# A third buffer for the output projection's weight halves, a bias rounded later, half of a rounding moved to GpSimd, and a first gather by feature groups

## What is computed

```python
y = _rms(y.reshape(...)) * out_norm_g
x = x + gate1 * (y @ w_out)                       # the output projection

h2 = rms_norm(x, norm2_g) * (1 + scale2) + shift2
logits = (xt @ router_w + router_b).astype(jnp.float32)
top_vals, top_idx = lax.top_k(logits, TOP_K)      # 4 of 32 experts
def expert_step(acc, params):
    u = xt @ w1 + b1
    glu = jnp.minimum(u[:, ::2], SWIGLU_LIMIT)
    lin = jnp.clip(u[:, 1::2], -SWIGLU_LIMIT, SWIGLU_LIMIT)
    a = glu * jax.nn.sigmoid(SWIGLU_ALPHA * glu) * (lin + 1)
    out = a @ w2 + b2
    return acc + gate_e[:, None] * out.astype(jnp.float32), None
```

## Time and profile before

| | |
|---|---|
| median of 3 runs | 1646.22 us (1643.47 to 1648.41) |
| the profiled execution | 1649.03 us, its span 1647.3 us |
| busy of the span | PE 93%, DVE 41%, ACT 28%, POOL 6% |
| moved by DMA | 534.24 MB, mean 324 GB/s |
| mean granted TensorE clock | 0.985 of full speed |

### The profile page before, as it was taken

How to read it: one execution, slowest core, us unless ns; L and a number is a source line. 1 busy time by engine, 2 the same in 40 slices (tenths; PEclk the granted TensorE clock), 3 DMA queues, 4 the chain that set the end, 5 groups by cost and what they waited for, 6 DMA issues and landing times. The chain is left out here.

```text
span 1647.3 us, 21485 instructions
## 1 busy us (share of the span) xinstructions
PE 1532.7 (93%) x8573; PEld 869.0 (53%) x8573; DVE 667.4 (41%) x960; ACT 454.0 (28%) x754; POOL 99.8 (6%) x114
## 2 busy tenths in 40 slices
PE   6999899999999988999998889886999999999998
PEld 3888633333333323333333323222858998789986
DVE  3576522232222222322221222223866565465654
ACT  3574411101111110111110101002865444354443
POOL 4032000000000000000000000000530000400000
PEclk8999899999999999999999999999999999999999
DMA  9977689999999999999999999999436555466540
GB/s 365 333 220 282 246 351 427 427 422 409 426 426 426 425 427 426 427 421 426 425 428 426 426 426 427 426 426 346 140 103 218 181 191 191 128 198 192 187 154 26
DMA packets 109695, 534.24 MB, mean 324 GB/s; under 512 B 6769, under 2 KB 69896, under 8 KB 83040
## 3 DMA queue, kind: packets, MB, share of 16 engines
q1 hardware_dynamic: 107600, 529.97, 81.1%
q0 software_dynamic: 1936, 1.98, 0.4%
HBM read 530.87 MB, written 1.05 MB: 323 GB/s over the span
## 5 line engine op out<-in xcount | busy, mean ns | idle before, releaser
L936 PE MATMUL ps<-ring,arena 128*64 128x512 f32 x2040 | 490.5, 606 | 21.8 <-DMA ring<-in_w_mlp 19.8
L936 PEld LDWEIGHTS ps<-ring,arena 128*64 128x64 f32 x2040 | 130.1, 137 | 261.7 <-issue 211.7
L954 PE MATMUL ps<-ring,arena 128*64 128x512 f32 x1024 | 230.9, 597 | 19.0 <-DMA ring<-in_w_mlp 11.6
L1546 DVE TENSOR_TENSOR wl<-ring,wh 128x1024 fp32r<-128x1024 f32 x132 | 162.0, 1232 | 135.2 <-ACT wh L2424 135.2
L541 PE MATMUL ps<-hth,wh 128*128 128x256 f32 x704 | 200.2, 284 | 1.9 <-DVE htl L2215 1.9
L542 PE MATMUL ps<-htl,wh 128*128 128x256 f32 x704 | 197.9, 281 | 0.0
L543 PE MATMUL ps<-hth,wl 128*128 128x256 f32 x704 | 197.3, 280 | 0.0
L2015 DVE TENSOR_TENSOR arena<-ps,arena 128x1024 f32<-128x1024 f32 x68 | 83.3, 1224 | 257.3 <-PE ps L961 250.6
L2424 ACT ACTIVATE wh<-ring 128x1024 fp32r<-128x1024 f32 x132 | 139.3, 1060 | 148.0 <-PE ps L543 148.0
L954 PEld LDWEIGHTS ps<-ring,arena 128*64 128x64 f32 x1024 | 74.1, 137 | 168.7 <-issue 142.3
L2040 DVE TENSOR_TENSOR arena<-ps,arena 128x512 f32<-128x512 f32 x34 | 23.5, 691 | 337.7 <-PE ps L954 334.5
(11 more groups left out here) (442 smaller groups left out, 1838.0 us busy)
## 6 DMA issues: line engine op xcount, KB each, us to landing
ring<-in_w_mlp SPq DMA_DIRECT2D x190, 2048.0 KB, 24.3
ring<-in_w_ada SPq DMA_DIRECT2D x24, 1024.0 KB, 11.0
ring<-in_ffn_w_gate SPq DMA_DIRECT2D x22, 1024.0 KB, 5.4
ring<-in_ffn_w_up SPq DMA_DIRECT2D x22, 1024.0 KB, 5.4
ring<-in_ffn_w_down SPq DMA_DIRECT2D x22, 1024.0 KB, 4.9
ring<-in_w_in SPq DMA_DIRECT2D x10, 768.0 KB, 12.2
ring<-in_w_in_ab SPq DMA_DIRECT2D x6, 1024.0 KB, 11.6
ring<-in_w_out SPq DMA_DIRECT2D x4, 1024.0 KB, 5.1
```

Source lines behind the costliest of these rows:

```text
L936: t = pe.matmul(PS[64 * g:64 * g + 64, HB[hb][ns], :], x[:, k8, :], u[:, f:f + 512], start=False, stop=k8 == 7)
L954: t = pe.matmul(PS[64 * g:64 * g + 64, 3, :], a4[:, kc, 64 * kg:64 * kg + 64], u[:, c, g * 512:(g + 1) * 512], start=k8 == 0, stop=k8 == 7)
L1546: dve.tensor_tensor(l, src, h.bitcast(F32), ALU.subtract).then_inc(*V.tick((st, "lo", n)))
```

## The change

Four edits:

- `out_bufs` gets a third pair of buffers, at `o_P + 1024`, which the mixer has left by then. `hi` of half n now waits for half n - 3.
- ACT rounds halves 2 to 5 in one run, then copies the gate row, then halves 6 and 7, and `B1S` behind them. DVE does its part of `B1S` behind half 7.
- `HL` of token tile 1 is written by GpSimd and no more by DVE: one instruction multiplies x by `rr[1]` into a new buffer `XR`, two subtract `HH`.
- The first gather goes by feature groups through the function `gather(b, kk, bank)`: groups 0 and 1 before the bias and `first_unit(0)`, groups 2 and 3 behind it. PE waits for all of `HL` before the first matmul.

```diff
         out_bufs = [tuple(rounded(f"wo{q}{n}", at_arena + 4 * (at + 1024 * n), 1024) for n in range(2))
-                    for q, at in enumerate((o_qk, o_ws + 2048))]
+                    for q, at in enumerate((o_qk, o_ws + 2048, o_P + 1024))]
...
             pe.wait_ge(*done(("ST", 0)))
             pe.wait_ge(*done(("HH", 1)))
-            for k in range(8):
-                for i in range(2):
-                    pe.matmul(PS[:, 4 + k // 2, (k % 2) * 256:(k % 2) * 256 + 256], HH[:, i, k * 128:(k + 1) * 128],
-                              ST[:, i, :], start=i == 0 and k % 2 == 0, stop=False)
-            for k in range(8):
-                for i in range(2):
-                    pe.wait_ge(*done(("HL", i)))
-                    t = pe.matmul(PS[:, 4 + k // 2, (k % 2) * 256:(k % 2) * 256 + 256], HL[:, i, k * 128:(k + 1) * 128],
-                                  ST[:, i, :], start=False, stop=i == 1 and k % 2 == 1)
-                if k % 2:
-                    t.then_inc(*P.tick(("gathered", 0, k // 2)))
+            for i in range(2):
+                pe.wait_ge(*done(("HL", i)))
+            gather(0, 0, 4)
+            gather(0, 1, 5)
...
             first_unit(0)
+            gather(0, 2, 6)
+            gather(0, 3, 7)
...
-            for n in range(2, 6):
+            for n in range(2, 8):
                 lo("out", n)
             for g in range(2):
                 p0 = 32 + 64 * g
                 dve.wait_ge(*done("B1H"))
                 dve.tensor_tensor(B1S[p0:p0 + 32, :], B1raw[p0:p0 + 32, :], B1S[p0:p0 + 32, :].bitcast(F32),
                                   ALU.subtract).then_inc(*V.tick("B1S"))
-            lo("out", 6)
-            lo("out", 7)
...
             dve.tensor_copy(most, cmax).then_inc(*V.tick("cnt"))
-            h_rest(1, 0, 1024)
             dve.wait_ge(*done("pos turned"))
...
-            hi("out", 2)
-            hi("out", 3)
+            for n in range(2, 6):
+                hi("out", n)
             for hf in range(2):
                 act.wait_ge(*done(("gate1", hf)))
                 act.activation(G1B[:, hf * 512:(hf + 1) * 512], PS[:, 6 + hf, :], ACT.Copy).then_inc(*S.tick(("G1B", hf)))
+            hi("out", 6)
+            hi("out", 7)
             act.wait_ge(s_load["b1"], 64)
             act.wait_ge(*done(("y turned", 3)))
             act.activation(B1S, B1raw, ACT.Copy).then_inc(*S.tick("B1H"))
-            for n in range(4, 8):
-                hi("out", n)
...
+            pool.wait_ge(*done(("x1", 1, 1)))
+            pool.wait_ge(*done(("rec", "n2", 1)))
+            pool.tensor_scalar(XR, X[:, 1, :], rr[1], None, ALU.mult).then_inc(*G.tick("XR"))
+            pool.wait_ge(*done("XR"))
+            pool.wait_ge(*done(("HH", 1)))
+            for c in range(2):
+                pool.tensor_tensor(apart(HL[:, 1, :], 0, 1024)[:, :, c, :], pairs(XR, 0, 1024)[:, :, c, :],
+                                   apart(HH[:, 1, :].bitcast(F32), 0, 1024)[:, :, c, :], ALU.subtract).then_inc(
+                    *G.tick(("HL", 1)))
```

More of the change, by code:

```diff
@@ L385, in build @@
         B1raw = v1(o_P + 3072, 1024)
+        XR = v1(o_P + 2048, 1024)
         HH, HL = (rounded_at(n, o, 2048).rearrange("p (t n) -> p t n", t=2)
```

## The result

| | before | with the change |
|---|---|---|
| median of 14 runs each, us | 1648.43 (1643.47 to 1651.76) | 1642.64 (1639.09 to 1645.53) |
| profiled execution, its span | 1649.03, 1647.3 | 1642.65, 1640.8 |
| mean granted clock | 0.985 | 0.986 |
| first product of half 0 | 156.53 | 156.74 |
| first quarter of x | 183.01 | 177.33 |

The ratio of the times is 0.9971 [0.9962, 0.998]: 0.29% faster, 4.8 us of 1648.43, with an interval (3.3 to 6.3 us) that lies on both sides of the 4.9 us that I had called the limit of what can be told. The forecast was 1642.2, which was 4.0 us less than the median of 1646.22 known then; that of before now came out 2.2 us higher.

What follows compares the result with a forecast made beforehand. Expert weight transfers were taken to bound the kernel, so its time follows the issue at 209.50 us. Terms -5.8 + 0 + 0 + 1.8 = -4.0 us, from 1646.22 to 1642.2 us; range 1638.8 to 1646.6.

Steps and rivals of the forecast that it cites:

- Term 1: Output projection: with PE's pauses at halves 4 and 7 gone, x starts at about 177.2 us, -5.8 us.
- The cover for `b1`: Output projection: the new order needs `b1` at 173.4 us; it landed at 168.9, 4.5 us of cover.
- rival D: Output projection: `b1` lands later as transfers share the DMA engines, eating the whole gain; 1646.2 us, chance 0.10.
- Terms 2 and 3: DVE losing `h_rest(1)` behind `ST`, and the gather's new order on PE: nothing on the chain waits, 0 each.
- Term 4: Routing: GpSimd's two subtractions shut out small DVE instructions, `ST` 1.8 us later; nothing charged for `XR`; +1.8 us.
- rival E: Gather: PE idles longer before it and its clock stays at half up to the issue; +2.7, 1648.9 us, chance 0.08.
- Rival B: Routing: GpSimd's work costs DVE nothing; -5.8, 1640.4 us, chance 0.15.
- rival C: Routing: `XR` shuts DVE out too, holding `h_rest` of tile 0, about +3.2; sum -2.6, 1643.6 us, chance 0.17.
- The row at 1402 us: Profile: a DVE subtraction took its normal 1.23 us beside a GpSimd multiply, so nothing was charged for `XR`.
- the rule of the sum: Expert stage: kernel time moves microsecond for microsecond with the expert transfer issued at 209.50 us before.

Runs made afterwards that it cites:

- r2: The kernel before with only the projection's part (third buffer, new order on ACT and DVE), GpSimd and gather as before: ratio 0.9957.
- r5: The kernel before with the third buffer alone, ACT and DVE in their old order: 1643.28 us.
- r6: The kernel before with the new order on ACT and DVE alone, two buffers: 1641.07 us.
- r4: The changed kernel with the old gather, first_unit(0) again behind all 32 gather matmuls: ratio 0.9961.
- r8: r4 with one more wait, so that GpSimd's two subtractions run behind `ST`, beside the gather: 1640.62 us.
- r9: r2 with four extra matmuls of unused result before PE's wait for the top 4, to keep PE awake: ratio 0.9954.
- r10: r2's program again, unchanged: ratio 0.9966.
- r1: The changed kernel again, as it is: ratio 0.9964.
- r3: The kernel before with only GpSimd's part (`XR`, two subtractions, DVE without h_rest(1)), projection and gather as before: ratio 1.0007.
- r7: The changed kernel with `XR` made by a GpSimd multiply of two tensor inputs instead of one by a scalar: 1642.81 us.

## Why the prediction held

**Term 1, the projection, -5.8: right.** x came 5.68 us earlier (5.89 counted), by the steps given: no pause at half 4, none at half 7, half 7's tiles and `B1S` meeting at 177.1 to 177.3. r2 shows it alone, r5 and r6 show both of its causes apart. That 2.0 us lay beyond the two pauses, from the half clock in 170 to 180 us, is right for most of it: PEclk went from 0.83 to 1.00. Before, the clock was at half from 172.1 to 175.5, over 3.3 us of PE's work, of which half, 1.6 us, was lost; where the other 0.4 comes from, I have not traced. The cover for `b1` held, so rival D fell.

**Terms 2 and 3, 0 and 0: right.** r4 shows the second directly, 48.45 against 48.43 and 48.75. The first was not tried by itself; in r8 `h_rest(1)` is away from DVE too and nothing on the chain before `ST` is shorter than in r2.

**Term 4, GpSimd, +1.8: the mechanism and the place right, the size a little low.** `XR` took 2.85 us where 2.9 was taken. The two instructions grew by 0.84 and 0.99 (1.06 and 1.21 against 0.22), where the text had 0.8 and 1.0. But from the reciprocal to `ST` the change is 2.22 us longer than before, 2.45 longer than r2. What the sum left out is PE's part of that chain, the places: three pairs of small matmuls between `chosen` and `ST`. From the last choice to DVE's next instruction they took 1.81 us in the change (191.28 to 193.09), 1.41 before. PE's timeline of the change there, and the window:

```profile
191.56 0.64 PE L890 MATMUL ps<-arena 128*128 128x32 f32 x2 [4.16 <-DVE arena L1952]
```
```profile
190.00:192.00 2.00, 0.43 (x2) 0.44 (x3) 1.93 (x5) 0.00 (x0) 1.17 (x1) 0.50 0.18 74
```

PE came out of a pause of 4.16 us, before 2.33, and the granted clock had already fallen to its half level, 1.2 GHz, in it. The step takes 1.17 to 1.23 us at the full clock (r2, r5, r6, r9), 1.4 where the clock falls within it (before, r10) and 1.81 at half. It was at half in all five profiles with the longer pause (the change, r1, r3, r4: 4.16 us, r7: 4.48), and once with the short one of 2.33 (r8). So the argument against rival E, that these matmuls "stay as they are", failed, in another place than E had: the half clock costs 0.4 us ahead of `ST`, not 6.7 behind it. That the longer pause brings it on is likely by these counts, but r8 shows that it isn't the only way. What the mis-sized term comes to at the issue lies between 1.4 and 3.2 us: 1.9 by r3 against before, 2.9 to 3.2 by the change and r1 against r2, 1.4 to 1.7 against r10.

**Rival B fell** (the subtractions cost what they were charged), and **rival C fell**: `h_rest` of tile 0 beside `XR` took 0.91 us, 0.87 before. The Trainium skill (page SBUF — State Buffer, section SBUF: two separate sides) says that a VectorE instruction with two SBUF inputs is fully blocked by a GpSimd instruction that reads SBUF and started before it. By that rule `XR` would hold `h_rest` in the change as it does in r7. It doesn't: the rule agrees with the trace for GpSimd's two-input instructions (1.26 us in place of 0.51 beside the multiply of r7, 1.06 and 1.21 in place of 0.22 beside the subtractions of the change), and does not hold for a multiply by one scalar for each row (2.85 us beside two DVE instructions of normal length). The row at 1402 us, by which the prediction decided, had told this right.

**From the gather on: not quite 1:1.** The clock behind the gather, on which E hung, did move the sum, in the other direction. From the gather's start to the issue before took 11.85 us, the change 11.07, because the full clock came back 2.6 us after the gather's start and not 5.1. The last two columns of the table bear this out: r9, with none of it at half, takes 9.66; each microsecond at half should add half of one, and 9.66 plus half of the last column gives 10.9 for r2 (10.65), 11.0 for the change (11.07), 11.5 for r1 (11.42), 12.2 and 12.3 for before and r10 (11.85, 11.89), and fits all twelve to 0.4 us. When the clock comes back differs between two profiles of one program (r2 and r10), so that these 0.8 us are not the change's.

**From the issue to the end: the rule is borne out.** This stretch took 1437.8 us before, 1435.7 with the change. Part of the difference stands at the end of the expert stage. PE's timeline of before there, and then that of the change:

```profile
1134.17 3.26 PE L954 MATMUL ps<-ring,arena 128*64 128x512 f32 x8 [0.62 <-ACT arena L2734]
...
1146.46 0.73 PE L1242 MATMUL ps<-obh,sgt 64*128 64x512 f32 x4 [3.09 <-DVEq L549]
```
```profile
1129.87 1.94 PE L955 MATMUL ps<-ring,arena 128*64 128x512 f32 x8 [0.62 <-ACT arena L2727]
...
1139.26 0.73 PE L1238 MATMUL ps<-obh,sgt 64*128 64x512 f32 x4 [1.79 <-DVEq L550]
```

Before ran part of its last expert at half clock and was 2.87 us longer from the issue to the first product behind the experts (936.96 against 934.09). No edit touches that, and it is not the change's. The same eight matmuls in r2, and in r10, which is the same program:

```profile
1127.86 1.94 PE L954 MATMUL ps<-ring,arena 128*64 128x512 f32 x8 [0.62 <-ACT arena L2732]
```
```profile
1128.94 3.46 PE L954 MATMUL ps<-ring,arena 128*64 128x512 f32 x8 [0.62 <-ACT arena L2732]
```

Over all twelve profiles the stretch from the issue to the end takes 1433.0 to 1437.8 us, and two profiles of one program lie up to 2.7 apart (1435.7 and 1433.0 of the change, 1435.8 and 1437.6 of r2's program). Cut in three, it shows where this comes from:

- From the issue to the last unit of the last expert's first layer (line 1094 of before), the stretch that the transfers set: 919.6 to 921.0 us in eleven profiles, though the issues themselves lie 9.6 us apart. Here the time moves with the issue, microsecond for microsecond, to 0.7 us. The exception is r9, with the earliest issue: 923.5, so that 3 us of its lead were lost among the expert transfers, within the first 290 us. Why, no run here shows.
- From there to the first product behind the experts: 13.65 us in eight profiles, 15.2 to 16.6 in before, r4, r9 and r10, where part of it was at half clock.
- From there to the end: 498.5 to 501.6 us, with no order that follows the edits (the change 501.6, r1 498.5).

The second and third pieces differ between two profiles of one program by as much as between kernels. So the rule of the sum held, and what the span of one profile adds to it is chance. The median of many runs is the better witness for the whole, and it gives 4.8 us (3.3 to 6.3) for a sum of 4.0.

**What of the hit was luck.** `ST` came 3.8 us earlier, counted, and not 4.0; the issue came 4.2 to 4.5 earlier because the clock returned sooner, which hid the 0.4 us that term 4 lacked. And that 1642.64 stands so near to 1642.2 owes something to the median of before, which was 1646.22 of three runs and then 1648.43 of fourteen: 4.0 us less than the latter is 1644.4. The range was looser than its terms, too: D plus 1.5 us of spread is 1647.7, C plus 1.5 is 1645.1, and the upper end of 1646.6 follows from neither.

**What stays open.** Whether the change or its projection part alone is faster in timed runs: medians of 1642.64 and 1641.39 against 1640.55 and 1641.21, intervals that overlap. The traces say that GpSimd's part makes `ST` 2.2 to 2.5 us later, and no run shows anything that it gives in return. Open, too, is why the full clock returns at another time in each execution, and why r9 lost 3 us behind the issue: kept awake, PE brings the issue forward, but one profile can't say that the kernel gains by it.

## What to carry to other kernels

Where an engine waits for a transfer in the middle of a row of copies, move the wait behind the copies first, and add the buffer second: here the order gave 3.1 us and the buffer 0.9, both 5.9. Before work goes to GpSimd because nobody there is busy, see which DVE instructions will run beside it: here a chain of small ones with two SBUF inputs paid 0.8 to 1.0 us for each two-input GpSimd instruction of 512 elements, and the work taken off DVE may never have been on the path. Read gains of this size from the length of a chain between two named events, not from absolute times, nor from the span of one profile.

## What the runs showed of the hardware

- A GpSimd multiply by one scalar for each row (128x1024, 2.85 us) leaves DVE's two-SBUF-input instructions at their normal length (0.91 us for two, 0.87 without it), and one with two tensor inputs (128x1024, 1.89 us, r7) held the one that started beside it until it was nearly over (1.26 us in place of 0.51). The chain that it stands beside was 0.33 us longer with the faster form (8.31 against 7.98).
- The form with two inputs, the second a broadcast column, is 0.96 us shorter than the form with a scalar, for the same product.
- With PE's pause of 2.3 to 4.5 us in the routing, the clock went to half (1.2 GHz) in it or within 2 us behind it in eleven of twelve profiles; with the four matmuls of r9 in it PE stayed at 1.00, 2.4 GHz, throughout, in one profile. In that program without them (r2, r10) the half clock reached 2.4 and 5.2 us into the gather.
